# Attention scores of the second block: heads by turns between two PSUM banks, decay products and masks behind them

## The chip, the cores and the metric

The kernel runs on one NeuronCore of a Trainium2 chip. TensorE (PE in the profile, its weight loads PEld) multiplies matrices into the eight banks of PSUM. VectorE (DVE), ScalarE (ACT) and GpSimd (POOL) do the rest, and the queue of SyncE (SP) issues nearly all DMAs. The metric is the time of one execution in microseconds on the device, lower is better.

## The reference, cut to what matters

A model of two blocks over 256 positions of width 1024. The first block mixes, attends to a memory, and runs a mixture of eight experts. The second block has two layers. Each layer has five attention groups of four heads, and a gated feed-forward part with a convolution. The change touches the scores of these attention groups:

```
o_a = _dense_causal_attention(q_a, k_a, v, MLA_QK_DIM ** -0.5)            # mla: 96 wide
o_b = _dense_causal_attention(q_b, k_b, v_b, HEAD_DIM ** -0.5, decay)     # fox: 64 wide, s + (cq - ck)
o_c = _moba_attention(q_c, k_c, v_c, HEAD_DIM ** -0.5)                    # moba: 64 wide, one causal block here
o_d = _diff_causal_attention(q_d[0], q_d[1], k_d[0], k_d[1], v, lam, ...) # diff: two maps, 32 wide each
o_e = _memory_attention(q_e, k_e, v_e, HEAD_DIM ** -0.5)                  # mem: 64 wide, no mask
x = x + concat(o_a, o_b, o_c, o_d, o_e) @ w_o
```

With 256 positions the moba group has a single block of keys, so it is plain causal attention. In each group but mem a causal mask is added to the scores before the softmax. In fox a decay term is added too.

## The kernel before, in words

Every engine has a program of its own, written out in order by hand. The engines meet only at semaphores. `pe_second` (line 1139), `act_second` (1907) and `dve_second` (3007) hold the order of one layer of the second block.

A quad (`quads`, line 2738) is four score maps for one tile of 128 queries. There are twelve in a layer: 0 and 1 are mla, 2 and 3 fox, 4 to 7 diff, 8 and 9 moba, 10 and 11 mem. A quad has `nk` keys: 128 for the first tile of queries, 256 for the second, always 256 for mem. Diff has two quads for each tile of queries, so quads 4 and 5 have 128 keys, and 6 and 7 have 256.

The heads of fox, moba and mem are taken in the order 0, 2, 1, 3. Transposed, heads 0 and 2 lie in partitions 0 to 63 and heads 1 and 3 in 64 to 127. So bank 0 of a quad (maps 0 and 1 of it) reads rows 0 to 63 of TensorE's array only, and bank 1 (maps 2 and 3) rows 64 to 127 only. In diff, bank 0 has the first map of each of two heads (32 rows), and bank 1 the second map (the 32 rows beside these). In mla each head has 96 rows.

`pe_scores` (line 1308) makes the scores of a quad. A query-key product is fp32 and stands in the trace as two weight loads and two matmuls. In fox each is followed by a decay product with all 128 rows (fp32r: one weight load and one matmul). Each bank ends with one mask product (line 1321, 128 rows, fp32r, identity by mask over both maps), and raises the bank's semaphore. Mem has no mask.

After the scores of quad n come, on PE, a part of the projections (`columns`, line 650) or of the output product (`product`, line 1370), then `pe_values` of quad n-1 (through `sum`, line 253), then the transposes of the exponentials of quad n (`pe_exp_turn`, through `pe_turn`, line 660), then the scores of quad n+1.

On DVE, `dve_max` (line 2847) reduces bank 0 when it is ready and bank 1 when it is ready (line 217), and forms the negated maximum (line 208 or 212). On ACT, `act_exp` then makes four exponentials (line 231). DVE also makes the low halves of all weights (line 205, `wL`), up to two blocks ahead, applies rotary embeddings and norms, and finishes the values of a quad (event `("o", n)`).

PSUM banks 4 to 7 go round in the order in which PE asks for them (`bank`, line 351). Asking waits until the last user of that bank is done. By the order of the calls, bank 0 of quad 7 is the one that the transposes of fox's output used: it is free when DVE has written `("fm_lo", "fox")`. Bank 1 of quad 7 is the one of the values of quad 5: it is free at `("o", 5)`. DVE makes these two one after the other, the first before the second. For the other quads from 2 on, bank 1 is freed by the exponentials of an earlier quad, by `("o", n-2)`, by the fm_lo of mla or by ACT's copy of a norm.

Of the kernel before, what the change touches and what calls it, by code (L numbers as in the profile page):

```python
# [14 lines left out]
S = 256  # L15
# [245 lines left out]
class Program:  # L261
# [1046 lines left out]
    def pe_scores(self, p, s, n, q):  # L1308

        for sig, event in q.ready:  # L1310
            p.wait_ge(*sig.of(event))
        p.wait_ge(*self.dve.of("masks"))
        for b in range(2):
            out = self.bank(p, (s, "S", n, b), self.act, (s, "exp", n, 2 * b + 1))[:, 0:2 * q.nk].rearrange("p (m k) -> p m k", m=2)
            first = True
            for m in range(2):
                for one, other in q.qk[2 * b + m]:
                    i = p.op.matmul(out[:, m, :], one, other, start=first, stop=False, skip_group_check=True)  # L1318
                    first = False
            if q.masked:  # L1320
                i = p.op.matmul(out[:, :, q.nk - 128:q.nk], self.ident_r[:, :],
                                self.mask_r[:, :].unsqueeze(1).broadcast_to([128, 2, 128]),
                                start=False, stop=True, skip_group_check=True)
            i.then_inc(*self.pe.up((s, "S", n, b)))

    def pe_exp_turn(self, p, s, n, q):

# [2152 lines left out]
```

## Time and profile before

| | us |
|---|---|
| median of 3 runs (2386.99 to 2393.14) | 2387.12 |
| the profiled execution's own time | 2385.82 |
| its span | 2383.9 |
| PE busy | 2336.1 (98%) |
| DVE busy | 1794.4 (75%) |
| ACT busy | 1370.1 (57%) |

The attention of the first layer of the second block lies at about 1686 to 1804 us of the span, that of the second layer at about 2061 to 2178 us. In a row of a timeline the first number is the start and the second the length, both in microseconds. Matmuls overlap, so the distance of two starts tells what one costs, and its own length doesn't.

### The profile page before, as it was taken

To read this page: it belongs to the slowest core of one execution; us is meant where nothing else is said; L and a number is where in the kernel's file an instruction comes from. 1 tells how busy PE (TensorE), PEld (TensorE's weight loads), DVE (VectorE), ACT (ScalarE), POOL (GpSimd) and SP (SyncE) were. 2 spreads that over 40 slices of the span, in tenths; PEclk is the share of its full clock that TensorE was granted. 3 is DMA by queue.
4 is the path that set the end of the run, shared out by engine and by line. 5 is a ranking of instruction groups with operands and counts; after the bars stand their busy time and mean duration, and the time that the engine had idled before them with its cause. 6 is when DMAs were issued, how large, how long until landed. Compare 5 with 4: busy or idle time off the path is not lost.

```text
span 2383.9 us, 33637 instructions
## 1 busy us (share of the span) xinstructions
PE 2336.1 (98%) x14448; PEld 2089.6 (88%) x14448; DVE 1794.4 (75%) x1835; ACT 1370.1 (57%) x1348; POOL 118.7 (5%) x94
## 2 busy tenths in 40 slices
PE   7999999999999999999999999999999999999999
PEld 7989999788988888888888888888889999888999
DVE  5856557675788888888888888887677676767665
ACT  5535445364577777777777776777455344645342
POOL 3001000001100000000000000000210001301000
PEclk9999999999999999999999999999999999999999
DMA  7644455453499999999999999996333655333553
GB/s 235 221 147 154 166 200 172 150 200 119 167 364 347 353 355 354 350 351 348 351 349 356 349 351 361 340 369 210 129 107 124 212 177 176 123 107 106 180 174 107
DMA packets 309691, 566.90 MB, mean 238 GB/s; under 512 B 12386, under 2 KB 137601, under 8 KB 309408
## 3 DMA queue, kind: packets, MB, share of 16 engines
q1 hardware_dynamic: 304752, 559.34, 66.4%
q10 hardware_dynamic: 4784, 5.35, 0.7%
q8 instruction: 115, 1.88, 0.3%
q14 instruction: 40, 0.33, 0.0%
HBM read 563.60 MB, written 1.05 MB: 237 GB/s over the span
## 4 chain that ended last, share of the span: by engine, by line
PE 87%; DVE 7%; DMA 3%; ACT 2%; issue 0%; POOL 0%; ACTq 0%; POOLq 0%; DVEq 0%
PE bank L1019 23%; PE bank L801 15%; PE bank L1037 11%; PE bank L650 9%; PE bank L785 7%; PE bank L638 6%; PE bank L253 5%; DVE wL L205 3%; PE bank L660 2%; ACT wH L234 2%; PE bank L1370 2%; PE bank L1318 2%; PE bank L626 1%; DMA raw<-in_od_moe_gu 1%; DMA raw<-in_ev_w_in 1%; DVE arena L205 1%
## 5 line engine op out<-in xcount | busy, mean ns | idle before, releaser
L205 DVE TENSOR_TENSOR wL<-raw,wH 128x2048 fp32r<-128x2048 f32 (+2 forms) x544 | 1210.4, 2233 | 351.0 <-ACT wH L234 348.0
L234 ACT ACTIVATE wH<-raw 128x2048 fp32r<-128x2048 f32 (+2 forms) x544 | 1014.7, 1867 | 498.8 <-PE bank L801 103.9
L1019 PE MATMUL bank<-wH,ra 128*128 128x512 f32 x1792 | 577.2, 393 | 1.2 <-DVE wL L205 0.9
L1019 PEld LDWEIGHTS bank<-wH,ra 128*128 128x128 f32 x1792 | 336.5, 188 | 71.9 <-issue 1.5
L801 PE MATMUL bank<-ra,wH 128*128 128x256 f32 x2112 | 383.6, 284 | 5.4 <-DVE ra L208 5.4
L1019 PE MATMUL bank<-wL,ra 128*128 128x512 f32 x896 | 348.7, 389 | 0.0
L801 PEld LDWEIGHTS bank<-ra,wH 128*128 128x128 f32 x2112 | 329.5, 192 | 8.1 <-DVE ra L208 6.9
L801 PE MATMUL bank<-ra,wL 128*128 128x256 f32 x1056 | 298.8, 283 | 0.0
L1037 PE MATMUL bank<-wH,ra 128*128 128x512 f32 x896 | 287.6, 391 | 0.3 <-DVE ra L205 0.2
L650 PE MATMUL bank<-wH,ra 128*128 128x512 f32 (+2 forms) x800 | 223.2, 361 | 0.5 <-DVE ra L208 0.5
L801 PEld LDWEIGHTS bank<-ra,wL 128*128 128x128 f32 x1056 | 202.7, 192 | 0.0
L1037 PEld LDWEIGHTS bank<-wH,ra 128*128 128x128 f32 x896 | 168.2, 188 | 37.1 <-DVE wL L205 1.6
L1019 PEld LDWEIGHTS bank<-wL,ra 128*128 128x128 f32 x896 | 168.5, 188 | 32.8
L638 PE MATMUL bank<-ra,wH 128*128 128x256 f32 x1056 | 192.0, 284 | 4.8 <-DVE arena L205 3.0
L785 PE MATMUL bank<-ra,wH 128*128 128x256 f32 x960 | 174.2, 283 | 0.2 <-DVE wL L205 0.2
L1037 PE MATMUL bank<-wL,ra 128*128 128x512 f32 x448 | 174.3, 389 | 0.0
L638 PEld LDWEIGHTS bank<-ra,wH 128*128 128x128 f32 x1056 | 164.9, 192 | 6.0 <-DVE arena L205 3.3
L650 PEld LDWEIGHTS bank<-wH,ra 128*128 128x128 f32 x800 | 147.7, 197 | 20.1 <-DVE ra L208 0.7
L785 PEld LDWEIGHTS bank<-ra,wH 128*128 128x128 f32 x960 | 149.7, 192 | 0.4 <-DVE wL L205 0.4
L638 PE MATMUL bank<-ra,wL 128*128 128x256 f32 x528 | 149.3, 283 | 0.0
L650 PE MATMUL bank<-wL,ra 128*128 128x512 f32 (+2 forms) x400 | 143.1, 358 | 0.0
L785 PE MATMUL bank<-ra,wL 128*128 128x256 f32 x480 | 135.8, 283 | 0.0
(212 smaller groups left out, 2558.9 us busy)
## 6 DMA issues: line engine op xcount, KB each, us to landing
raw<-in_od_moe_gu SPq DMA_DIRECT2D x224, 1024.0 KB, 6.3
raw<-in_od_moe_down SPq DMA_DIRECT2D x112, 1024.0 KB, 6.6
raw<-in_ev_ffn_gu SPq DMA_DIRECT2D x22, 1024.0 KB, 5.1
raw<-in_ffn_w_gate SPq DMA_DIRECT2D x22, 1024.0 KB, 5.4
raw<-in_ffn_w_up SPq DMA_DIRECT2D x22, 1024.0 KB, 5.1
raw<-in_ffn_w_down SPq DMA_DIRECT2D x22, 1024.0 KB, 4.8
raw<-in_xa_wkv SPq DMA_DIRECT2D x16, 1024.0 KB, 5.3
raw<-in_od_pw_w SPq DMA_DIRECT2D x12, 1024.0 KB, 5.0
```

The costliest lines, as they stand in the source:

```text
L205: self.op.tensor_tensor(out, a, b, op).then_inc(*self.sig.up(name))
L234: self.op.activation(out, a, ACT.Copy, **kw).then_inc(*self.sig.up(name))
L253: m = self.op.matmul(out, a, b, start=i == 0, stop=i == len(pairs) - 1)
L638: m = p.op.matmul(out, a, b, start=c == 0 and i == 0, stop=c == k - 1 and i == 2)
L650: m = p.op.matmul(outs[t][:, 0:wd], a, b, start=half == 0 and c == 0 and i == 0, stop=half == 1 and c == 3 and i == 2)
L660: m = p.op.transpose(out[place], part, self.ident[0:count, 0:count])
L785: m = p.op.matmul(self.banks[nb // 2][:, (nb % 2) * 256:(nb % 2) * 256 + 256], a, b, start=q == 0 and c == 0 and nb % 2 == 0 and i == 0, s ...
L801: m = p.op.matmul(out[:, j * 256:j * 256 + 256], a, b, start=c == 0 and i == 0 and not (j and by_chunk), stop=c == C - 1 and i == 2, skip_ ...
L1019: m = p.op.matmul(out[:, :], a, b, start=half == 0 and c == 0 and i == 0, stop=half == 1 and c == 3 and i == 2)
L1037: m = p.op.matmul(self.banks[n][:, :], a, b, start=f == 0 and half == 0 and c == 0 and i == 0, stop=f == NRD - 1 and half == 1 and c == 1 ...
L1318: i = p.op.matmul(out[:, m, :], one, other, start=first, stop=False, skip_group_check=True)
L1370: m = p.op.matmul(self.banks[nb // 2][:, (nb % 2) * 256:(nb % 2) * 256 + 256], one, other, start=first and c == 0 and nb % 2 == 0 and i == ...
```

## The change

For every group but mla, both banks of a quad are asked for ahead of its first matmul. Then the maps go by turns between the banks: bank 0 map 0, bank 1 map 0, bank 0 map 1, bank 1 map 1. In fox the four decay products follow after all four query-key products. Then come both masks, each raising its bank's semaphore. Mla keeps one bank after the other. In mem, which has no mask, the last product of each bank raises its semaphore. No product is added or left out.

```
-        for b in range(2):
-            out = self.bank(p, (s, "S", n, b), self.act, (s, "exp", n, 2 * b + 1))[:, 0:2 * q.nk].rearrange("p (m k) -> p m k", m=2)
-            first = True
-            for m in range(2):
-                for one, other in q.qk[2 * b + m]:
-                    i = p.op.matmul(out[:, m, :], one, other, start=first, stop=False, skip_group_check=True)
-                    first = False
-            if q.masked:
-                i = p.op.matmul(out[:, :, q.nk - 128:q.nk], self.ident_r[:, :],
-                                self.mask_r[:, :].unsqueeze(1).broadcast_to([128, 2, 128]),
-                                start=False, stop=True, skip_group_check=True)
-            i.then_inc(*self.pe.up((s, "S", n, b)))
+        for some in ((0,), (1,)) if q.g == "mla" else ((0, 1),):
+            out = {b: self.bank(p, (s, "S", n, b), self.act, (s, "exp", n, 2 * b + 1))[:, 0:2 * q.nk].rearrange("p (m k) -> p m k", m=2)
+                   for b in some}
+            for term in range(len(q.qk[0])):
+                for m in range(2):
+                    for b in some:
+                        one, other = q.qk[2 * b + m][term]
+                        i = p.op.matmul(out[b][:, m, :], one, other, start=term == 0 and m == 0, stop=False, skip_group_check=True)
+                        if m and not q.masked:
+                            i.then_inc(*self.pe.up((s, "S", n, b)))
+            for b in some if q.masked else ():
+                p.op.matmul(out[b][:, :, q.nk - 128:q.nk], self.ident_r[:, :],
+                            self.mask_r[:, :].unsqueeze(1).broadcast_to([128, 2, 128]),
+                            start=False, stop=True, skip_group_check=True).then_inc(*self.pe.up((s, "S", n, b)))
```

## Rows read from the trace of the kernel before

**Rows 1.** The page: busy time of the engines, and the chain that ended last.
```profile
PE 2336.1 (98%) x14448; PEld 2089.6 (88%) x14448; DVE 1794.4 (75%) x1835; ACT 1370.1 (57%) x1348; POOL 118.7 (5%) x94
...
PE 87%; DVE 7%; DMA 3%; ACT 2%; issue 0%; POOL 0%; ACTq 0%; POOLq 0%; DVEq 0%
```
**Rows 2.** Timeline of PE, first layer, quad 3 (fox, 256 keys).
```profile
1711.95 0.70 PE L1318 MATMUL bank<-arena 64*128 64x256 f32 x2
1712.58 0.38 PE L1318 MATMUL bank<-ra 128*128 128x256 f32 x1
...
1713.74 0.28 PE L1321 MATMUL bank<-maskR,identR 128*128 128x256 f32 x1
1713.95 0.70 PE L1318 MATMUL bank<-arena 64*128 64x256 f32 x2
...
1715.74 0.28 PE L1321 MATMUL bank<-maskR,identR 128*128 128x256 f32 x1
1715.86 0.60 PE L660 MATMUL bank<-cst,arena 128*128 128x128 f32 x4
```
**Rows 3.** Timeline of PE, first layer, quad 2 (fox, 128 keys): first and last row.
```profile
1699.66 0.49 PE L1318 MATMUL bank<-arena 64*128 64x128 f32 x2
...
1702.43 0.41 PE L1321 MATMUL bank<-maskR,identR 128*128 128x256 f32 x1
```
**Rows 4.** Timeline of PE, first layer, quad 7 (diff, 256 keys) and what follows.
```profile
1747.16 1.13 PE L1318 MATMUL bank<-arena 32*128 32x256 f32 x4
1748.21 0.39 PE L1321 MATMUL bank<-maskR,identR 128*128 128x256 f32 x1
1748.53 1.13 PE L1318 MATMUL bank<-arena 32*128 32x256 f32 x4
1749.59 0.39 PE L1321 MATMUL bank<-maskR,identR 128*128 128x256 f32 x1
1749.81 0.28 PE L650 MATMUL bank<-wH,ra 128*128 128x256 f32 x1
```
**Rows 5.** Timeline of PE, first layer, quad 4 (diff, 128 keys).
```profile
1724.03 0.71 PE L1318 MATMUL bank<-arena 32*128 32x128 f32 x4
1724.66 0.38 PE L1321 MATMUL bank<-maskR,identR 128*128 128x256 f32 x1
...
1725.84 0.60 PE L660 MATMUL bank<-cst,arena 128*128 128x128 f32 x4
```
**Rows 6.** Timeline of PE, first layer, quad 10 (mem, 256 keys).
```profile
1783.40 1.14 PE L1318 MATMUL bank<-arena 64*128 64x256 f32 x8
1784.47 0.51 PE L1370 MATMUL bank<-ra,wH 128*128 128x256 f32 x2
```
**Rows 7.** Timelines of DVE: quad 7's second maximum (first layer); quads 6 to 7 (second layer).
```profile
1750.01 0.69 DVE L217 TENSOR_REDUCE small<-bank 128x2 f32<-128x512 f32 x1 [0.51 <-PE bank L1321]
...
2115.13 0.69 DVE L217 TENSOR_REDUCE small<-bank 128x2 f32<-128x512 f32 x1 [0.68 <-PE bank L1321]
...
2120.82 0.68 DVE L205 TENSOR_TENSOR ra<-bank,ra 128x512 fp32r<-128x512 f32 x1
...
2122.06 0.29 DVE L205 TENSOR_TENSOR arena<-arena 128x128 f32<-128x128 f32 x1
```
**Rows 8.** Timeline of PE: the matmuls that follow three of its waits for DVE.
```profile
1776.74 0.66 PE L660 MATMUL bank<-cst,arena 128*128 128x128 f32 x4 [2.59 <-DVE arena L205]
...
2121.55 1.31 PE L1318 MATMUL bank<-arena 32*128 32x256 f32 x4 [1.44 <-DVE ra L205]
...
2151.88 0.66 PE L660 MATMUL bank<-cst,arena 128*128 128x128 f32 x4 [1.80 <-DVE arena L205]
```
**Rows 9.** Stretches: length, busy time of PE, PEld, DVE, ACT, POOL, granted clock, DMA share, GB/s.
```profile
1702.50:1705.90 3.40, 3.40 (x10) 2.75 (x10) 2.95 (x9) 1.51 (x8) 0.00 (x0) 0.50 0.13 14
...
1750.30:1753.70 3.40, 3.40 (x19) 3.40 (x18) 3.37 (x4) 2.66 (x9) 0.00 (x0) 0.50 0.02 5
...
2122.40:2129.20 6.80, 6.80 (x25) 5.34 (x24) 4.80 (x8) 2.35 (x9) 0.00 (x0) 0.50 0.01 3
```

## The prediction

> **What bounds the kernel.** I read the page first. PE is busy for 98% of the span and makes 87% of the chain that ended last [rows 1]. So an interval that PE loses or gains is on the path, except where PE itself waits. I then read the timeline of PE through both attention stages, and looked for starts that lie further apart than the matmul before them needs. In quads 2 to 6 there are no waits for another engine: the distances inside a quad are TensorE's own. Three waits of more than a microsecond come later [rows 8]. One ends at the scores of quad 7 in the second layer. The two others (1776.74, 2151.88) end at the transposes of diff's output, after the scores of quad 9. At the scores of quad 7 in the first layer PE is hardly later than DVE, and there its clock was slow just before.
>
> Inside a quad the rows show where time goes. A 256-key query-key product has two matmuls 0.32 us apart at first, then 0.22 us. In quad 3 the decay product starts 0.63 us after the head does, so 0.31 us after the second matmul, not 0.22 (1711.95, 1712.58) [rows 2]. After a mask that follows a short-row product, the next short-row product starts 0.32 us later (1748.21 to 1748.53), while a mask's own 256 columns need 0.12 us (1715.74 to 1715.86) [rows 2, 4]. So each change between products of 32 or 64 rows and products of 128 rows costs 0.1 to 0.2 us. Mem, which has no such change inside, shows something else: eight matmuls of 256 columns, and what follows starts 1.07 us after the first (1783.40 to 1784.47) [rows 6]. Four such matmuls of diff, all in one row group, need 1.05 us until their mask starts [rows 4]. So rows 0 to 63 and 64 to 127 already work at the same time in mem, with bank 0's two heads ahead of bank 1's in the program. What keeps the other quads from it is the mask (and decay product) between the banks.
>
> **The change, part by part.** First the length of each quad on PE, from its first matmul to the next engine work.
>
> *256 keys, diff and moba.* Before: 1747.16 to 1749.81 = 2.65 us [rows 4]. After: the two row groups side by side, first mask at 1.05 us, second mask 0.22 us later (as 1749.59 to 1749.81), the next work 0.12 us after that: 1.40 us with 0.01 for the shift between the groups. Saved: 1.25.
>
> *128 keys, diff and moba.* Before: 1724.03 to 1725.84 = 1.81. After: first mask at 0.63, then 0.22 and 0.12: 0.98. Saved: 0.83 [rows 5].
>
> *Fox, 256 keys.* Before: 3.91 (1711.95 to 1715.86). After: first decay product at 1.06, the second 0.22 later, then two more decay products, two masks and the next work, each 0.12: 1.88. Saved: 2.03 [rows 2].
>
> *Fox, 128 keys.* Before: 1699.66 to 1702.43 plus 0.22 = 2.99. After: 0.64, 0.22, five times 0.12: 1.46. Saved: 1.53 [rows 3].
>
> *Mem* keeps its length, since its halves run side by side now. Mla keeps its order.
>
> Of the 64-row groups the side by side run is measured [rows 6]. For two 32-row groups (diff) no row shows it. Bounds: as in mem (the values above), or not at all. Then the first mask comes four matmuls later (4 x 0.22, or 4 x 0.11 with 128 keys), and each diff quad saves 0.39. I take mem's behaviour, the nearest rows, since the row groups are disjoint in the same way. The Trainium skill says in TensorEngine Tiling (Tiling Modes, Key Properties) that different tiles can load and multiply in parallel, and lists 32-row tiles beside 64-row ones. By it the sum below is 14.3, without it 9.1; no run here has shown it for 32 rows.
>
> The order inside a pair is weighed too. The row group of bank 1 starts with bank 0's second head still to come [rows 6]. The Trainium skill, TensorE: Matmul & The Clock Gate (Part 3, The mechanism), calls matmuls strict first in, first out, in start and end. By that rule mem would overlap only where the groups meet, and the turns would save about 0.6 us in each of four mem quads, 2.5 us more in all. The row disagrees with it, and I count nothing for mem.
>
> Now what of this is on the path, in one layer. Quads 2, 3, 4 and 5: PE waits for nothing before or behind them, so all counts: 1.53 + 2.03 + 0.83 + 0.83 = 5.22. The exponentials of these quads are done before PE asks for them (no wait of PE at their transposes), and weights are split two blocks ahead.
>
> Quad 6 counts by DVE, not by PE. Behind its maxima DVE works without a pause (a weight block, moba's rotary embedding, the low half of fox's output) until 2121.50, and only that frees quad 7's bank 0 (2115.13 to 2120.82 + 0.68) [rows 7]. PE waits for it [rows 8]. Here the order of masks costs something: both maxima now stand behind both masks. Before, the second maximum starts 2.85 us after the quad (1747.16 to 1750.01), with the first long done [rows 4, 7]. After, the first mask starts at 1.05, its maximum 0.42 later, and the second maximum some 0.65 behind it: 2.1 to 2.2. So 0.70 of 1.25 reaches DVE.
>
> Quad 7 has an added wait. Both banks are asked for at its start, and bank 1 is free only when DVE has finished `("o", 5)`: 2122.35 instead of 2121.50, 0.85 us later [rows 7]. Behind it on PE stand the whole quad and then the columns. It starts 0.85 later and is 1.25 shorter: +0.40. For the other quads the same wait costs nothing that I can see. `("o", n-2)` needs 0.4 to 0.8 us on DVE, and PE has 0.44 or 0.87 us of transposes between. Quad 8 is the closest, at about 0.05 us.
>
> Quad 8: 0.83, on the path, with PE running through to the values of quad 7. Quad 9: 1.25 shorter, but PE then waits for DVE's chain from the values of quad 7 to diff's norm, and that chain had no pause for quad 9's scores. The wait grows (1.8 us idle in the second layer) and the gain is nothing [rows 8]. Quads 10 and 11: nothing.
>
> Sum of a layer: 5.22 + 0.70 + 0.40 + 0.83 = 7.15. Two layers: 14.3 us.
>
> **The clock.** In the two attention stages seven stretches of 3.4 us have a granted clock of 0.50, the level of 1.2 GHz. Three places stand in the rows: 3.4 us right after quad 2, 3.4 us behind quad 7, and 6.8 us from quad 7 of the second layer on, the last after a wait of 1.44 us [rows 8, 9]. Each 3.4 us on the path costs 1.7. Ahead of all three stand scores with few rows at work, or an idle PE. The change makes the scores denser and shorter, which may keep the clock up after quad 2. It also makes the waits at quad 7 and before diff's output longer by 0.3 to 1.3 us each, which may pull it down. From minus three to plus three stretches, 5 us each way. I take 0, as the two push against each other.
>
> The profiled execution's own time is 2385.8; less 14.3 it is 2371.5. The median of the runs shown is 1.3 us above it, so I forecast 2372.8.
>
> **Rivals.** (a) The 32-row groups don't run side by side. Quads 4 and 5 then save 0.39 each. At quad 6 the second maximum starts at 1.92 + 0.42 + 0.65 = 2.99 instead of 2.85: -0.14. Quad 7: 0.39 - 0.85 = -0.46. With fox and quad 8 that is 4.54 a layer, 9.1 in all: 2378.0. For it: no row. Against: mem.
>
> (b) DVE takes over after quad 3. In the 3.4 us behind quad 7 it is busy for 3.37 [rows 9], and with a shorter PE part it may end last. Then only fox's savings remain, 3.56 x 2 = 7.1: 2380.0, just at no change. Against it: DVE is at 75% over all, and in those 3.4 us it is ahead of PE's needs.
>
> (c) More clock: up to three slow stretches vanish from the path, 5.1 us more: 2367.7. Quad 2's is the likeliest.
>
> (d) Slower than before: the clock. Longer waits at quads 7 and 9, and shorter matmul bursts, make the granted clock fall in many more places of the attention stages. Each costs 1.7, so nine cancel the gain (8.4 x 1.7 = 14.3), and thirteen make it slower by 0.3%: 2394. Before, there are seven. Against it: the work around the scores is dense, and PE is full in all of quads 2 to 6.
>
> **Numbers.** The forecast 0.57, (a) 0.15, (b) 0.10, (c) 0.13, (d) with milder forms of it 0.05. What a measurement here tells from no change is about 0.3%, 7.2 us. Faster by more: 0.57 + 0.15 + 0.13 and a little of (b) = 0.87. Within: 0.10. Slower: 0.03. The range 2366 to 2380 takes in (a), (c) and the edge of (b).
>
> **What would show it.** Right: eight matmuls of L1318 in one row for diff and moba, as for mem, with the next work 1.4 us (256 keys) or 1.0 us (128) behind the first; fox at 1.9 and 1.5; two maxima of DVE back to back; quad 7 starting 0.85 us later after fm_lo than before; a wait ahead of diff's output that is over a microsecond longer; the attention stages about 7 us shorter each and all else unchanged. Wrong: diff's first mask at 1.9 us (then (a)); gaps of PE in front of the transposes of the exponentials (then (b)); a count of slow-clock stretches that differs by more than three from before.

## The result, and the profile after

The changed kernel takes 2377.4 us (median of 5 runs, 2374.6 to 2385.1), the kernel before 2389.6 (5 runs). The ratio is 0.9945, with a 95% interval of 0.9924 to 0.9965. So the change saves about 13 us by the ratio (the two medians differ by 12.2); 14.3 were forecast. The forecast time was 2372.8 us. The measured one is 4.6 us above it, and 2.5 of these lie in the kernel before, whose median rose from 2387.1 us (3 runs) to 2389.6 (5 runs). The profiled executions differ by less, 2372.8 us of span against 2383.9. The rest of the program, which has no edit, is 1.9 us slower in this one. Up to the first scores it takes 1689.6 us instead of 1686.6. A stretch of 3.4 us at a granted clock of 0.50 from 1652.4 us on, which the execution of the kernel before doesn't have, may be part of this. In seven later executions of variants this part takes 1691 to 1697 us. Only e6 and e7 change anything in it (DVE's decay copies come ahead of the first scores), so most of this spread isn't the programs'. From the end of the second attention stage to the end it is 1.1 us shorter. I compare the two attention stages by themselves, from the first scores to the first gate or up matmul of the feed-forward part (line 801):

| stage | before | after | difference |
|---|---|---|---|
| first layer | 126.4 | 120.6 | -5.8 |
| second layer | 125.1 | 118.0 | -7.2 |

What lies between them, the feed-forward part and the second layer's first projections, takes 248.5 us in both. The page after (spans, busy time, the chain), which answers to [rows 1]:

```profile
span 2372.8 us, 33645 instructions
...
PE 2317.1 (98%) x14448; PEld 2079.6 (88%) x14448; DVE 1791.6 (76%) x1835; ACT 1370.0 (58%) x1348; POOL 119.4 (5%) x94
...
PE 85%; DVE 7%; DMA 4%; ACT 3%; issue 0%; POOL 0%; ACTq 0%; DVEq 0%; POOLq 0%
```

The timeline of PE after, first layer: quad 2, quad 3, quad 4 and quad 6, each with what follows. It answers to [rows 2 to 5], with quad 6 in place of quad 7, since quad 7 is slowed by its clock after the change. Line 1320 holds the products, 1324 the masks.

```profile
1704.17 0.72 PE L1320 MATMUL bank<-arena 64*128 64x128 f32 x8
1704.81 0.66 PE L1320 MATMUL bank<-ra 128*128 128x128 f32 x4
1705.31 0.45 PE L1324 MATMUL bank<-maskR,identR 128*128 128x256 f32 x2
1705.60 0.39 PE L650 MATMUL bank<-wH,ra 128*128 128x512 f32 x1
...
1713.35 1.13 PE L1320 MATMUL bank<-arena 64*128 64x256 f32 x8
1714.41 0.74 PE L1320 MATMUL bank<-ra 128*128 128x256 f32 x4
1714.99 0.40 PE L1324 MATMUL bank<-maskR,identR 128*128 128x256 f32 x2
1715.23 0.38 PE L660 MATMUL bank<-cst,arena 128*128 128x128 f32 x2
...
1723.38 0.71 PE L1320 MATMUL bank<-arena 32*128 32x128 f32 x8
1724.03 0.50 PE L1324 MATMUL bank<-maskR,identR 128*128 128x256 f32 x2
1724.37 0.49 PE L660 MATMUL bank<-cst,arena 128*128 128x128 f32 x3
...
1735.41 1.13 PE L1320 MATMUL bank<-arena 32*128 32x256 f32 x8
1736.47 0.51 PE L1324 MATMUL bank<-maskR,identR 128*128 128x256 f32 x2
1736.82 0.49 PE L660 MATMUL bank<-cst,arena 128*128 128x128 f32 x3
```

Eight matmuls now stand in one row, and their last starts where the fourth stood before. From start to the next work, quad 2 takes 1.43 us (2.98 before), quad 3 1.88 (3.91), quad 4 0.98 (1.81), quad 6 1.41 (2.65 in the second layer).

What PE waits for after, in both layers: at quad 7, at the transposes of mem's heads behind quad 9, and at diff's output. It answers to [rows 8]:

```profile
1744.86 2.08 PE L1320 MATMUL bank<-arena 32*128 32x256 f32 x8 [2.85 <-DVE arena L205]
...
1767.51 0.66 PE L660 MATMUL bank<-cst,arena 128*128 128x128 f32 x4 [0.70 <-DVE smb L223]
...
1773.94 0.55 PE L660 MATMUL bank<-cst,arena 128*128 128x128 f32 x3 [2.91 <-DVE arena L205]
...
2113.75 2.08 PE L1320 MATMUL bank<-arena 32*128 32x256 f32 x8 [2.85 <-DVE arena L205]
...
2136.28 0.66 PE L660 MATMUL bank<-cst,arena 128*128 128x128 f32 x4 [0.70 <-DVE smb L223]
...
2141.93 0.44 PE L660 MATMUL bank<-cst,arena 128*128 128x128 f32 x2 [2.12 <-DVE arena L205]
```

The four on `arena` from L205 are longer than before. At quad 7 it is 2.85 us instead of 0.1 in the first layer and 2.85 instead of 1.44 in the second. At diff's output it is 2.91 instead of 2.59, and 2.12 instead of 1.80. The two of 0.70 us weren't there before. DVE after, second layer, from the maxima of quad 6 to those of quad 7, which answers to [rows 7]:

```profile
2105.78 1.29 DVE L217 TENSOR_REDUCE small<-bank 128x2 f32<-128x512 f32 x2
...
2112.06 0.68 DVE L205 TENSOR_TENSOR ra<-bank,ra 128x512 fp32r<-128x512 f32 x1
...
2113.31 0.29 DVE L205 TENSOR_TENSOR arena<-arena 128x128 f32<-128x128 f32 x1
...
2116.38 1.29 DVE L217 TENSOR_REDUCE small<-bank 128x2 f32<-128x512 f32 x2 [1.82 <-PE bank L1324]
```

Both maxima are in one row. Quad 7 starts at 2113.75, after `("o", 5)` at 2113.60. fm_lo of fox was done at 2112.74.

The stretches of slow clock after, columns as in [rows 9]:

```profile
1693.40:1696.80 3.40, 3.40 (x18) 3.40 (x17) 2.99 (x3) 1.51 (x8) 2.68 (x1) 0.50 0.16 56
1744.60:1751.40 6.80, 6.54 (x29) 5.81 (x30) 4.91 (x9) 2.39 (x9) 0.00 (x0) 0.50 0.04 17
1775.30:1778.70 3.40, 3.40 (x19) 3.40 (x18) 0.66 (x1) 0.00 (x0) 0.00 (x0) 0.51 0.58 202
2062.10:2065.50 3.40, 3.40 (x19) 3.40 (x18) 3.37 (x4) 1.72 (x9) 3.11 (x1) 0.50 0.26 93
2113.30:2120.10 6.80, 6.35 (x28) 5.62 (x29) 4.89 (x9) 2.20 (x9) 0.00 (x0) 0.50 0.07 25
```

There are seven of 3.4 us, as before. None follows fox now. In the first layer one came up behind quad 0, between whose banks PE is idle for 1.73 us in the kernel before and 1.74 in this one. At quad 7 of the first layer it is two in a row, and they cover the quad itself.

### The profile page after: what moved, and what is told of

It reads as the page before. It is cut to its first block, busy times and chain, and to the rows that moved or that the text cites. A ratio compares the mean times of both kernels' runs of the same rounds, so it can differ in the third digit from the quotient of the medians.

```text
span 2372.8 us, 33645 instructions
## 1 busy us (share of the span) xinstructions
PE 2317.1 (98%) x14448; PEld 2079.6 (88%) x14448; DVE 1791.6 (76%) x1835; ACT 1370.0 (58%) x1348; POOL 119.4 (5%) x94
## 3 DMA queue, kind: packets, MB, share of 16 engines
q8 instruction: 115, 1.88, 0.3%
## 4 chain that ended last, share of the span: by engine, by line
PE 85%; DVE 7%; DMA 4%; ACT 3%; issue 0%; POOL 0%; ACTq 0%; DVEq 0%; POOLq 0%
PE bank L1019 22%; PE bank L801 15%; PE bank L1037 11%; PE bank L650 9%; PE bank L785 7%; PE bank L638 6%; PE bank L253 5%; DVE wL L205 3%; DMA raw<-in_od_moe_gu 2%; ACT wH L234 2%; PE bank L660 2%; PE bank L1372 2%; PE bank L626 1%; PE bank L1320 1%; DVE arena L205 1%; DMA raw<-in_od_moe_down 1%
## 5 line engine op out<-in xcount | busy, mean ns | idle before, releaser
L205 DVE TENSOR_TENSOR wL<-raw,wH 128x2048 fp32r<-128x2048 f32 (+2 forms) x544 | 1209.0, 2232 | 349.6 <-ACT wH L234 347.1
```

The costliest lines, as they stand in the source:

```text
L205: self.op.tensor_tensor(out, a, b, op).then_inc(*self.sig.up(name))
```

## The experiments

My theory: what kept the two row groups apart was the full-row product between them (mask or decay), and each change between short-row and full-row products costs TensorE 0.1 to 0.2 us. The change removes both. What is missing of its full length is swallowed by PE's waits for DVE at quad 7 and before diff's output. The rivals: that it is the turns between the banks that save; that the waits don't matter and the clock alone does. All stage times below are from one profiled execution each. Where a variant leaves a quad and its clock alone, its length agrees within 0.03 us between kernels. The first four variants have a single timed run each: 2382.4 us (e1), 2384.8 (e2), 2371.9 (e3) and 2366.3 (e4), with 2391.8 for the kernel before beside them. Since the part up to the first scores differs by up to 7 us between executions, I go by the stages.

**e1_bank_by_bank**: the turns undone, the rest of the change kept.

```
             for term in range(len(q.qk[0])):
-                for m in range(2):
-                    for b in some:
+                for b in some:
+                    if term == 0:
+                        out[b] = self.bank(...)      # bank 1 is asked for here, not ahead of all
+                    for m in range(2):
```

> The changed kernel, but the two maps of bank 0 come first, then bank 1 is asked for, then its two maps; the decay products and both masks stay behind all of them. My theory (the mask and decay products between the banks were what kept the row groups apart, the turns themselves matter little): every quad as long as in the changed kernel, 1.41 us (256 keys, diff and moba), 0.98 (128), 1.88 and 1.43 (fox), within 0.05. Quad 7's first bank starts when fm_lo of fox is done, 0.85 us earlier than in the changed kernel, its second bank 0.85 us later, and the mask comes no earlier. Rival (turns are needed, matmuls go strictly in order): the two banks overlap only where they meet, the 256-key quads take about 2.0 us, the attention stages are 3 to 5 us longer.

Measured: 1.44, 1.89, 0.99, 0.99 and 1.41 us for quads 2 to 6, so as with turns. The stages take 120.4 and 117.9 us (120.6 and 118.0 with turns). Timeline of PE, second layer, quad 7:

```profile
2119.50 2.92 PE L1321 MATMUL bank<-arena 32*128 32x256 f32 x8 [1.90 <-DVE ra L205]
2122.36 0.80 PE L1325 MATMUL bank<-maskR,identR 128*128 128x256 f32 x2
2122.95 0.41 PE L650 MATMUL bank<-wH,ra 128*128 128x256 f32 x1
```

Quad 7 starts after a wait of 1.90 us, for `ra` (fm_lo of fox), instead of 2.85 for `arena` (`("o", 5)`), 7.09 us behind quad 6 instead of 8.04. It is then 0.85 us longer, 3.45 instead of 2.60. So the added wait is real, and it costs only 0.1 us by itself: without it quad 7 starts 0.95 us sooner, but ends just 0.1 us sooner, since its second bank comes free no earlier. The turns between banks change nothing. For diff and moba e1 differs from the kernel before in one thing alone, the place of bank 0's mask, and a quad of 256 keys goes from 2.65 to 1.41 us. So the placement of the full-row products is the change.

**e2_decay_between**: the decay products back between the query-key products.

```
-            for term in range(len(q.qk[0])):
-                for m in range(2):
-                    for b in some:
-                        one, other = q.qk[2 * b + m][term]
+            for m in range(2):
+                for b in some:
+                    for term, (one, other) in enumerate(q.qk[2 * b + m]):
```

> The changed kernel, but in fox each head's decay product follows its own query-key product at once (turns between banks and masks behind as in the change). My theory: each decay product has all 128 rows and so parts the row groups again. Fox with 256 keys takes about 3.7 us (four times 0.94), with 128 keys 2.7 to 2.8, against 1.88 and 1.43 in the changed kernel; the other quads stay at 1.41 and 0.98. Rival (it is the turns between banks that save, wherever the decay products are): fox stays near 1.9 and 1.5.

Measured: fox takes 2.88 us (128 keys) and 3.91 us (256 keys), against 2.94 to 2.98 and 3.91 in the kernel before, although both masks stand behind all products here. The other quads keep 0.98 and 1.41. Timeline of PE, second layer, quad 3, beginning and end:

```profile
2089.07 0.70 PE L1319 MATMUL bank<-arena 64*128 64x256 f32 x2
2089.70 0.38 PE L1319 MATMUL bank<-ra 128*128 128x256 f32 x1
2090.01 0.70 PE L1319 MATMUL bank<-arena 64*128 64x256 f32 x2
2090.64 0.38 PE L1319 MATMUL bank<-ra 128*128 128x256 f32 x1
...
2092.74 0.40 PE L1323 MATMUL bank<-maskR,identR 128*128 128x256 f32 x2
2092.98 0.38 PE L660 MATMUL bank<-cst,arena 128*128 128x128 f32 x2
```

Two heads in different row groups and different banks, and yet 0.94 us apart, as two heads of one bank were in the kernel before. My 3.7 was 0.2 too low, my 2.8 by 0.1. The stages take 124.0 and 121.4 us, 3.4 us more than in the changed kernel in both. So fox's part is about half of the 7.15 forecast for a layer. In all these runs the two short-row groups also write two different banks, so it isn't shown whether the overlap needs both. Different banks alone don't give it: the full-row decay products of the changed kernel go by turns between the banks, 0.12 us apart, which is what 256 columns need in one bank too.

**e3_rotary_late**: DVE's order ahead of quad 7.

```
-        self.dve_rope_norm(v, s, l, "moba", 64, 1)
         self.dve_out_turned(v, s, "fox")
         value(5)
         turned(6)
+        self.dve_rope_norm(v, s, l, "moba", 64, 1)
         top(7)
```

> The changed kernel, but DVE does moba's rotary embedding and norm behind the values of quad 5 and the copies of quad 6, not ahead of fox's low half. Both events on which quad 7 waits (fm_lo of fox, o of quad 5) come about 2.8 us earlier. My theory: PE's wait ahead of quad 7 (2.8 us in the changed kernel) shrinks to under 0.8 us, each layer is 2.0 to 2.8 us shorter by that, and the slow clock of 6.8 us that begins at quad 7 becomes shorter or goes, which gives another 1.7 to 3.4 us a layer. Rival 1 (the clock falls for the sparse scores, not for the wait): the slow stretches stay, only 2 to 2.8 us a layer. Rival 2: the rotary embedding, now ahead of quad 7's maxima, delays its exponentials so that PE waits before their transposes, and nothing is gained.

**e4_norm_early**: DVE's order ahead of diff's output.

```
+        self.dve_sub_norm(v, s, l)
         final_norm(2)
         blocks("w_o", l, "fox")
-        self.dve_sub_norm(v, s, l)
```

> The changed kernel, but DVE does diff's norm ahead of the final norm's two chunks and of a weight block (0.87 us and 2.28 us), not behind. My theory: the wait of PE before diff's output is transposed (3.1 us in the first layer, 2.3 in the second, by the distance of the starts less what the matmul needs) goes down to under 0.4 us, so quad 9's saving is on the path now: 2.7 us in the first layer and 2.0 in the second. Rival: the weight block that comes later, or the low half of diff's output behind it, makes PE wait at the next place, and under 1 us a layer is left.

Timelines of PE: quad 7 in e3, second layer.

```profile
2110.62 1.13 PE L1320 MATMUL bank<-arena 32*128 32x256 f32 x8 [0.92 <-DVE arena L205]
2111.68 0.51 PE L1324 MATMUL bank<-maskR,identR 128*128 128x256 f32 x2
2112.02 0.28 PE L650 MATMUL bank<-wH,ra 128*128 128x256 f32 x1
```

In e3 the wait goes from 2.85 to 0.92 us, and quad 7 takes 1.41 us instead of 2.60, since the clock is no longer slow there. The stages: 117.4 and 116.4 us, 3.2 and 1.5 less than in the changed kernel. The wait is near the size that I expected (under 0.8 us), but the sum is below the 3.7 to 6.2 us that I expected in both layers. The gap behind quad 7 stays at 8.3 us although its clock is full. By the list of waits PE now loses 0.8 us before the values of quad 6 (for ACT's exponentials, rival 2 in part), and 0.7 at quad 8. And in the second layer a slow stretch came up behind the wait at diff's output (the gap ahead of quad 10 is 13.6 us, was 12.1). That wait is 2.11 us long, and the changed kernel has the same one (2.12 us) with no slow stretch behind it.

In e4 the gap ahead of quad 10 is 9.93 us in both layers, was 14.41 and 12.13: 4.5 and 2.2 less, where 2.7 and 2.0 were expected. The 1.8 more in the first layer go with the slow stretch at 1775 us, which is gone. PE's 2.91 and 2.12 us of waiting there are gone too. The stages take 114.6 and 112.9 us. This also has 1.5 us each from a slow stretch behind quad 0 that this execution didn't have, and in the second layer 1.35 us at quad 7, where the wait is as long as ever and the quad still ran at full clock. Only one stretch followed, behind it. Timeline of PE, and the stretch (columns as in [rows 9]):

```profile
2108.66 1.13 PE L1320 MATMUL bank<-arena 32*128 32x256 f32 x8 [2.84 <-DVE arena L205]
```

```profile
2110.70:2114.10 3.40, 3.40 (x18) 3.40 (x18) 3.37 (x5) 2.44 (x9) 0.00 (x0) 0.50 0.00 0
```

**e5_both**: both moves together.

> The changed kernel with both moves on DVE: the rotary embedding of moba later, and diff's norm earlier. My theory (two waits of PE held gains back, and the clock fell for them): each layer as short as the two moves apart make it: gap ahead of quad 7 6.1 us, gap ahead of quad 10 9.9 us, quad 7 1.4 us long. First layer 117.4 - 4.5 = 112.9 us or less, second 116.4 - 2.2 - 1.5 (clock) = 112.7. Rival: the two moves overlap in what they give (both only move the clock's slow stretches), and a layer stays at 114 to 115.

Measured: 111.5 and 112.7 us, as expected within 0.1 in the second layer, and 1.4 better in the first, where no stretch of slow clock is left at all. These 1.4 us are the stretch behind quad 0, which this execution has in the second layer only, so nothing that the moves did. The rival fell. The single run took 2367.1 us, with 1696.3 us up to the first scores.

**e7_decay_early**: e5, and DVE's decay copies ahead of diff's squares.

```
         self.dve_turned(v, s, l, "mla")
+        self.dve_decay(v, s)
         self.dve_mean_heads(v, s, "diff", sqh[:, :], 32)
         blocks("in", l, "fox_v", 1)
         columns("fox_v")
-        self.dve_decay(v, s)
         top(0)
```

> e5 plus DVE's copy of the decay sums (two instructions) right behind mla's transposed keys, ahead of diff's sums of squares, a weight block and the copy of fox's values. Bank 1 of quad 0 waits for it (2.1 us between the starts in all kernels so far). My theory: that wait goes down to under 0.4 us, each layer is 1.7 us shorter than in e5, and one slow stretch less near it, so a layer of about 111 us and a time 0.9 to 1.1% under the kernel before. Rival: the next thing that quad 0 or its maxima need is late by as much (DVE reaches quad 0's maxima no earlier), so quad 1 and the gap ahead of it grow by what quad 0 loses.

The rival was right for the waits. Quad 0 takes 1.13 us instead of 3.12, but the gap behind it grows from 3.31 to 5.13 us. PE now waits for the exponentials of quad 0. Timelines of PE and of ACT, first layer:

```profile
1700.46 0.44 PE L660 MATMUL bank<-cst,sq 128*128 128x128 f32 x2 [1.62 <-ACT sq L231]
```

```profile
1697.01 1.28 ACT L231 ACT_TABLE_LOAD   x1
1698.90 0.37 ACT L231 ACTIVATE sq<-bank,small 128x128 f32<-128x128 f32 x1 [0.60 <-DVE small L212]
```

DVE reaches quad 0's maxima no earlier, behind the same weight block (the first starts 3.24 us behind the quad's first product; in e5 it was 2.43), so 0.2 of 2.0 us is left. The stages take 111.3 and 111.1 us. Neither has a slow stretch: in the second layer that is 1.5 us against e5. So the layers and the time came out as I expected, but by the clock: of the 1.7 us that the shorter wait was to give, 0.2 came. Two stretches of this kernel, first and second attention stage, columns as in [rows 9]:

```profile
1694.70:1806.00 111.30, 104.93 (x833) 97.17 (x831) 81.96 (x156) 58.89 (x136) 12.48 (x4) 1.00 0.35 111
2054.50:2165.60 111.10, 104.74 (x831) 96.97 (x829) 78.92 (x148) 58.66 (x135) 12.48 (x4) 1.00 0.35 111
```

Over 4 runs its median is 2365.4 us, against 2389.4 of the kernel before (7 runs): ratio 0.9896 (0.9879 to 0.9912). Its interval lies below that of the changed kernel, 0.9945 (0.9924 to 0.9965). It has the lowest time here, but e4 and e5 with a single run each (2366.3 and 2367.1 us) are too close to be told from it.

**e6_moves_alone**: the scores as in the kernel before, with the same three moves as e7.

> The kernel before (its order of scores) with the same three moves on DVE as in e7. My theory: with no wait of PE to swallow it, the change of the scores is worth its full length on PE: 1.53 + 2.03 + 0.83 + 0.83 + 1.25 + 1.25 + 0.83 + 1.25 = 9.8 us a layer, so each layer here is some 9.8 us longer than in e7 (give or take 1.7 for a slow stretch), against 7.15 between the kernel before and the changed one. Rival: DVE takes over once PE is that quick, and e7 and this one differ by no more than 7 us a layer.

Measured: 120.5 and 118.4 us, so 9.2 and 7.3 us more than e7. The quads are 9.8 us longer in sum, as expected, but the rival holds in part. In the second layer e7 gives back 1.0 us ahead of quad 7 (a gap of 6.11 against 5.11), 1.1 ahead of quad 10 and 0.4 ahead of quad 8: DVE and ACT come last there again. One thing goes the other way: e6 has three slow stretches in the two stages (at 1712.7, 1750.3 and 2125.7 us, behind quads 2, 6 and 7, with no wait ahead of them), e7 has none. The gap ahead of quad 8 parts the two effects. In the first layer e6 has no slow stretch there, and e7 gives back 1.66 us instead of 0.4. So at full clock e7 gives back 3.7 us a layer, and my estimate from these gaps is that the change of the scores is then worth 9.8 - 3.7 = 6.1 us a layer, within the rival's 7. The rest of the 9.2 and 7.3 is the clock, 3.1 and 1.2 us. The time is 2377.5 us, ratio 0.994 (0.9924 to 0.9957). So the three moves alone are worth about as much as the change alone, and together they give close to the sum of both.

The clock of the whole program points the same way over several runs. Its mean granted value is 0.992 to 0.995 in seven runs of the kernel before, 0.992 to 0.994 in five of the changed kernel, 0.996 or 0.997 in four of e6, and 0.998 or 0.999 in four of e7. It also holds stretches outside the attention stages. By it the change alone left the clock as it was, the moves raised it, and with the moves in place the change raised it further.

## Why the prediction was right

*Lengths on PE.* Forecast and measured: fox with 128 keys 1.46 and 1.43, with 256 keys 1.88 and 1.88, the others 0.98 and 0.98, 1.40 and 1.41. Adding up distances of starts from the rows before was enough.

*32-row groups side by side.* Taken over from mem's 64-row groups, and right: eight matmuls of diff start within the time of four. Rival (a) fell, and so did the price without this rule (9.1 us; its sum for a layer is 4.57 us, not the 4.54 written there, which changes nothing). The Trainium skill's page TensorEngine Tiling (Array Packing), in Tiling Modes, Key Properties, lets the 32-row tiles run in parallel; the trace agrees (1.06 us from the first of eight to the mask).

*Nothing for mem.* Right: 1.06 to 1.07 us in all kernels. The strict order of TensorE: Matmul & The Clock Gate (Part 3, The mechanism), in the Trainium skill, doesn't hold across row groups here: in quad 10 of the kernel before, bank 0's four matmuls stand ahead of bank 1's four in the program, and the eight start in pairs 0.01 us apart, the first pair at 1783.40 and the fourth 0.75 us later. e1, with bank 0's matmuls all ahead of bank 1's, is as fast as the turns.

*Quads 2 to 5.* 5.22 us a layer forecast. The second layer gives 1.51 + 2.03 + 0.83 + 0.83 = 5.20, with the gaps between them unchanged to 0.02.

*Quad 6 and the added wait at quad 7.* Forecast: quad 7 starts 0.15 us later relative to quad 6 than before (0.85 less 0.70). Measured in the second layer: 0.17. In the first, where the clock was slow before, it starts 0.02 us sooner. The wait for `("o", 5)` shows by name after, and e1 parts it off.

*Quad 9.* Nothing forecast, and nothing came: the quad is 1.25 shorter, and the gap behind it 1.25 to 1.26 longer. But the sign that I gave, a wait ahead of diff's output over a microsecond longer, didn't show. That wait grew by 0.32 us. The rest goes at a place that I had overlooked: the new wait at the transposes of mem's heads (1767.51, 2136.28), for DVE's copy of line 223, in both layers. The starts of the transposes around it lie 0.98 and 0.17 us apart, where it was 0.11 each before, which is 0.93 us more. (My list of waits over a microsecond also left out the 1.59 us ahead of line 801 at the end of both stages. It is the same after.)

*The clock: the term that was mis-sized.* I took 0, with the waits at quad 7 and diff's output growing by 0.3 to 1.3 us each. At quad 7 they grew by 1.4 and 2.7 us. The count of slow stretches stayed at seven, but they moved to worse places in the first layer. Before, quad 7 there ran at full clock (2.65 us). After, the stretches begin with the quad and it takes 2.60, so its saving of 1.25 is gone but for 0.05. The gap behind it is 0.38 longer. Fox's stretch went (1.56 back), and one came behind quad 0 (1.49 lost). Quad 7 starts 0.17 us sooner behind quad 6 than forecast, and is 1.20 longer. Together: 1.20 + 0.38 + 1.49 - 1.56 - 0.17 = 1.34, and 7.15 - 5.80 = 1.35 us are missing in the first layer. In the second, where both kernels are slow at quad 7, the sum is 7.17 against 7.15. That it is so close is in part luck: at half clock quad 7 saves 1.53 us instead of 1.25, and the gap behind it is 0.23 longer. e3, e5 and e7 show the tie to the wait: with PE's idle time at quad 7 down to 0.9 us the stretches there are gone in both layers (six of six). After 1.4 to 2.9 us of it there is one or two each time (nine of nine), but where they begin isn't fixed: in e4's second layer only behind the quad. The old scores had them even without a wait (1750.3 us before [rows 9], and three in e6). What decides on the stretch behind quad 0 isn't settled: e4 had none in either layer and e5 one in the second alone, the changed kernel and e1 in both, with the same wait at quad 0 and, in the first layer, the same program up to there.

*Rivals.* (b) was wrong for quads 4 to 8 as they stand, but e3, e5 and e7 show DVE and ACT as the next bound behind the waits. (c) and (d) didn't come; the thirteen stretches of (d) would make 2394.9 us, not 2394.

## What to carry to other kernels

Put the matmuls that use only part of TensorE's rows next to each other, and those that need all rows behind them. The order among the short ones didn't matter here, with up to four matmuls of one row group ahead of the other's. Then look at what waits for another engine behind the shortened part: here two moves in DVE's order, with no work removed, took 4.1 to 4.8 us a layer from PE's waits, of which some 1.5 us came back at other waits, and at quad 7 the slow clock behind the wait went too.

## What the runs showed that I had not expected

A fast part can cost clock: the same quad 7 took 2.65 us at full clock with all its work in line, and 2.60 at half clock with its work side by side, after PE had idled 2.85 us ahead of it. With 0.92 us of idle time there it took 1.40 (e3). And the order of a pair's matmuls in the program didn't decide which ran together: in e1 four matmuls of one row group stand ahead of four of the other, and they overlap as fully as in turns.
